# Normalising, projecting and attention in one program, a head's query tile ahead of its gate tile, and the first query tiles loaded under the last gate

## The chip, the core and the metric

The kernel runs on one core of a Trainium2 chip. The core has TensorE (PE, matmuls), VectorE (DVE), ScalarE (ACT), GpSimd (POOL) and SyncE (SP, which here only issues DMAs). Each engine runs its own instructions in order and waits for the others through semaphores. The metric is the device time of one execution in microseconds; the less the better.

## The reference

One inference step of a two-layer streaming encoder, for a prompt of 1024 tokens and a sample of 32 tokens behind 512 cached ones, with a model width of 1024. Layer 0 is what this change touches:

```python
hn = rmsnorm(h, norm_w[0])
q, k, v, z, qi, ki, wi = split_cols(hn @ w_in, ...)     # 8 query heads, 2 key heads, 8 index heads of 128
q, k, qi, ki = rope(q), rope(k), rope(qi), rope(ki)
score = einsum('bth,bths->bts', wi * IDX_SCALE, relu(qi . ki))   # one score per (token, key)
_, sel = top_k(where(admissible, score, -inf), n_sel)            # 256 keys (136 for the sample)
probs = softmax(where(valid, q . k[sel] * ATT_SCALE, -inf))
h = h + ((probs @ v[sel]) * silu(z)) @ w_out
```

Layer 1 is a gated linear recurrence with its own projections, and a last RMSNorm follows. Outputs are both groups' results, the keys, values and index keys, and the recurrent states. All is float32; each large product is made of three passes (high x high, high x low, low x high parts).

## The kernel before

Tokens lie in nine tiles of 128 (`NT` = 9, the last with the 32 sample tokens). The kernel is a series of programs, each an `nc.Block`, in which every engine has its own list of instructions. At the end of a block all engines wait for one another before the next begins. The first block, `norm_and_project`, runs `input_norm` and `attention_project`; the second is `attention`; the third, `out_and_recur`, is the output projection and the recurrence; the fourth is `final_out`.

`attention_project` goes through `TILES`, 27 column tiles of 128: index keys, 8 index queries, 2 key tiles, and then for each head a gate tile (`Z0`) and a query tile (`Q0`). A tile has three units of 352 tokens; a unit is one product of 24 matmuls into one of four PSUM banks (line 187). TensorE may start unit i when ScalarE has read unit i-4 (line 611), and VectorE too where it reads it. What happens to a unit depends on its kind:

- "gate": ScalarE applies Silu and writes it to `gT` (line 675).
- "q": ScalarE makes two half copies and one full one (lines 667, 668, 672; the full one waits until the store of the unit two before it has landed). GpSimd multiplies with sine and cosine (721, 724) and adds (710), the addition of a unit behind the multiplications of the next. SP then stores it to the DRAM tensor `q_rotated` (547).
- "rope" (index and key tiles): as "q", but VectorE multiplies with the cosine and the result stays in SBUF.

Between the two key tiles lie the "score" units. When the scores are there, VectorE searches the selection threshold of each token, bit by bit: `BITS` = 31 rounds of `search`, each of a proposal (line 802), counts over five tiles (793), and a decision (808, 809). The counts of the two widest tiles are made by ScalarE with Sign and an accumulator (`count_signs`, line 651), which waits for the proposal; the decision waits for both. `next_float` (821 to 834) ends the search. ScalarE's rounds stand in its instruction list among the reads of the units, at places that a table fixes when the program is built:

```python
BITS, PACE = 31, 6000
...
    if i > rope_last:
        time += 3850
        counted_after[i] = min(BITS, time // PACE)
```

`rope_last` is the last unit of the second key tile; 48 units, those of the gates and queries, follow it. After the first gate tile the key rows are also transposed and stored, one tile of tokens at every third unit (`rows_before`).

`attention` goes over 72 items (token tile, head). TensorE makes the logits (line 941) from the query tile, VectorE subtracts, masks and finds the minimum (`shift`, line 1027), ScalarE applies Exp (1067), VectorE divides (1035, 1037), TensorE transposes (954), ScalarE copies (1077), TensorE multiplies with the values (970), VectorE applies the gate (1043). SP loads the query tile of each token tile from `q_rotated` (line 913) into one of two places, tiles 0 and 1 at the block's start, a later tile t when the logits of tile t-2 are done; the raw output weights follow the load of tile 3 (918). These places lie in the region of `hn_lo`, which the projection reads to its end.

Of the kernel before, what the change touches and what calls it, by code (L numbers as in the profile page):

```python
# [25 lines left out]
P = 128  # L26
# [20 lines left out]

TILES = [KI0] + [QI0 + P * i for i in range(IH)] + [K0 + P * i for i in range(KVH)]
for _i in range(HEADS):
    TILES += [Z0 + P * _i, Q0 + P * _i]  # L50
RH, DK, DV = 8, 128, 128
REC_Q, REC_F, REC_V, REC_Z = range(4)

# [34 lines left out]
def build(nc, io):  # L88
    with ExitStack() as ctx:
# [42 lines left out]
        S["w_raw"] = space("w_raw", [P, W_SLOTS, KT, P])  # L132
        S["w_lo"] = Space(nc, w_at)("w_lo", [P, W_SLOTS, KT, P], F32R)
        S["w_hi"] = space("w_hi", [P, W_SLOTS, KT, P], F32R)
        S["cos"] = space("cos", [P, T])
        S["sin"] = space("sin", [P, T])

# [15 lines left out]
        S["raw_in"] = [sem(f"raw_in{i}") for i in range(W_SLOTS)]  # L153
        S["w_hi_done"], S["w_lo_done"] = sem("w_hi"), sem("w_lo")
        S["tables_in"], S["cache_in"] = sem("tables_in"), sem("cache_in")
        norm_and_project(nc, S, space)
        attention(nc, S)
        out_and_recur(nc, S)
        final_out(nc, S)

# [95 lines left out]
    return score[:, 0:PAST // P * 384].rearrange("p (b c) -> p b c", b=PAST // P)  # L256


def norm_and_project(nc, S, space):
    swapped = space("swapped", [P, 3, CW])  # L260
    relu = space("relu", [P, 2, 512])
    S["wi"] = space("wi", [P, NT, IH])
    S["kiTs"] = space("kiT_sample", [P, KEYS_S])
    S["signs"] = space("signs", [P, D], BF16)
    S["swapped"], S["relu"] = swapped, relu
    first, later = input_norm(nc, S), attention_project(nc, S)
    with nc.Block() as block:
        @block.sync
        def _(sp):
            first["sync"](sp)  # L270
            later["sync"](sp)

        @block.tensor
        def _(pe):
            first["tensor"](pe)
            later["tensor"](pe)

        @block.scalar
        def _(act):
            first["scalar"](act)  # L280
            later["scalar"](act)

        @block.gpsimd
        def _(pool):
            first["gpsimd"](pool)
            later["gpsimd"](pool)

        @block.vector
        def _(dve):
            first["vector"](dve)  # L290
            later["vector"](dve)


def input_norm(nc, S):
# [154 lines left out]
def attention_project(nc, S):  # L449
# [86 lines left out]
    if True:  # L536
        def sync(sp):
            def load(c):
                if c >= SLOTS:
                    sp.wait_ge(acc_ready, last_of_tile[c - SLOTS] + 1)  # L540
                sp.dma_start(raw[:, c % SLOTS], w_in[:, :, tiles[c]:tiles[c] + P]).then_inc(raw_in[c % SLOTS], 16)

            def store_q(c, parts):
                for i, (kind, tile, part, head) in enumerate(units):
                    if kind == "q" and tile == c and part in parts:
                        sp.wait_ge(rope_done, n_rope[i + 1])
                        sp.dma_start(q_dram[head, :, part * CW:(part + 1) * CW],
                                     relu[:, n_q[i] % 2, 0:CW]).then_inc(q_stored[n_q[i] % 2], 16)
# [12 lines left out]
            for c in range(SLOTS, len(tiles) + SLOTS):  # L561
                store_q(c - SLOTS, (0,))
                if c < len(tiles):
                    load(c)
                store_q(c - SLOTS, (1, 2))

                if c == SLOTS:
                    sp.wait_ge(v_read, NT)
                    sp.dma_start(io["v_prompt"][0, 0].rearrange("(t p) h d -> p t (h d)", p=P), v[:, 0:SAMPLE, :]).then_inc(v_stored, 16)
                    sp.dma_start(io["v_sample"][0, 0].rearrange("t h d -> t (h d)"), v[0:DEC, SAMPLE, :]).then_inc(v_stored, 16)  # L570
                for i in range(done, last_of_tile[c - SLOTS] + 1):
                    if i in rows_before:
# [300 lines left out]
def attention(nc, S):  # L873
# [29 lines left out]
    space = Space(nc, S["lo_at"])  # L903
    probs = space("probs", [P, RING, SEQ])
    low = space("low", [P, 3, N])
    q = space("q_tile", [P, 2, HEADS, P])
    with nc.Block() as block:
        @block.sync
        def _(sp):
# [11 lines left out]
        @block.gpsimd  # L921
        def _(pool):
# [4 lines left out]
        @block.tensor  # L927
        def _(pe):
            def multiply(i):
                t, h = items[i]  # L930
                n = keys(t)
# [2 lines left out]
                if i >= 2:  # L934
                    pe.wait_ge(logits_read, i - 1)
                if h == 0:
                    pe.wait_ge(q_in[t % 2], 16 * (t // 2 + 1))
                src = kTs if t == SAMPLE else kT
                for a in range(0, n, 512):
                    e = min(n, a + 512)  # L940
                    last = pe.matmul(logits[0:rows(t), i % 2, a:e], q[:, t % 2, h, 0:rows(t)],  # L941
                                     src[:, h // GROUP, a:e], start=True, stop=True)
                last.then_inc(logits_ready, 1)

# [13 lines left out]
            def mix(g, quarter):  # L958
# [8 lines left out]
                for j in range((n * quarter + 3) // 4, (n * (quarter + 1) + 3) // 4):  # L967
# [5 lines left out]
                    if j == n - 1:  # L973
                        last.then_inc(mixed, 1)

            for i in range(N + LAG + 4):
                if i < N:
                    multiply(i)
                if 0 <= i - LAG < N:
# [1 line left out]
                if i >= LAG + 4:  # L981
                    mix((i - LAG - 4) // 4, (i - LAG) % 4)

        @block.vector
        def _(dve):
            n_order = 0

            def link(instruction):
# [51 lines left out]
            def gate(g):  # L1040
# [3 lines left out]
                                  ps[2 + g % 2][:, 0:4 * rows(t)].rearrange("p (g q) -> p g q", g=4),  # L1044
                                  gT[:, h:h + 4, span(t)], ALU.mult).then_inc(gated, 1)

            for i in range(N + 12):
                if i < N:
                    t, h = items[i]
# [7 lines left out]
                if i >= 12 and i % 4 == 0:  # L1057
                    gate((i - 12) // 4)

        @block.scalar  # L1060
        def _(act):
            for i in range(N + LAG):
                if i < N:
                    t, h = items[i]
# [15 lines left out]
                if i in (6 * HEADS, 7 * HEADS):  # L1080
                    act.wait_ge(wo_in, 64)
                    out_weights_hi(act, S, i // HEADS - 6)


def out_and_recur(nc, S):
# [913 lines left out]
```

## Time and profile before

| | |
|---|---|
| median of 3 runs | 1477.39 us (1475.63 to 1477.44) |
| the profiled execution | 1477.57 us |
| its span, first to last instruction | 1475.8 us |
| TensorE busy / weight loads | 1386.3 us (94%) / 1204.5 us |
| VectorE, ScalarE, GpSimd busy | 926.5, 640.2, 553.7 us |
| mean granted TensorE clock | 0.983 of full |
| projection's last stage (gates and queries) | about 255 to 442 us |
| attention | about 456 to 650 us |

The times in the views are microseconds from the first instruction. Busy times are of compute instructions alone. The granted clock is 1.00 at 2.4 GHz and 0.50 at 1.2 GHz.

### The profile page before, as it was taken

What the parts mean: (1) busy time and instruction counts of PE and PEld (TensorE: products, weight loads), DVE (VectorE), ACT (ScalarE), POOL (GpSimd) and SP (SyncE); (2) the same over time, 40 slices, a digit from 0 to 9 for tenths busy, and PEclk for the clock granted to TensorE, in tenths of its full rate; (3) what the DMA queues carried; (4) which work ended last, traced back from release to release, by engine and by line L of the source; (5) the groups of instructions that cost most, each with busy time, mean ns of one, the idle gap of its engine ahead of it and who ended that gap; (6) DMA issues with size and microseconds to landing.
All of it is one profiled execution on the core that took longest, in us unless ns stands there. A gap on an engine that the chain in (4) does not pass through costs nothing. (4 is left out here: it accounts for less than half of the span.)

```text
span 1475.8 us, 21147 instructions
## 1 busy us (share of the span) xinstructions
PE 1386.3 (94%) x8028; PEld 1204.5 (82%) x8028; DVE 926.5 (63%) x1702; ACT 640.2 (43%) x1123; POOL 553.7 (38%) x399
## 2 busy tenths in 40 slices
PE   5999999999995999999989999999999999997998
PEld 5999746999993455458879998989898989996786
DVE  4211388869887988644568484848484848486233
ACT  4433365677764556531225352525252525252121
POOL 2466601464641001000025373737373737373000
PEclk9999999999997999999999999999999999999899
DMA  6211100223203310002231111111111111105221
GB/s 222 93 45 44 43 1 15 70 74 90 75 30 113 101 29 4 1 29 86 90 87 46 29 35 44 35 44 35 44 35 44 35 44 35 44 6 206 100 86 64
DMA packets 95316, 86.80 MB, mean 59 GB/s; under 512 B 5585, under 2 KB 83281, under 8 KB 95217
## 3 DMA queue, kind: packets, MB, share of 16 engines
q1 hardware_dynamic: 93584, 80.63, 17.6%
q0 software_dynamic: 1632, 4.82, 0.9%
q8 instruction: 66, 1.08, 0.3%
q14 instruction: 34, 0.27, 0.1%
HBM read 65.46 MB, written 19.97 MB: 58 GB/s over the span
## 5 line engine op out<-in xcount | busy, mean ns | idle before, releaser
L187 PE MATMUL bank<-hn_hi,rw_hi 128*128 128x352 f32 x768 | 251.1, 327 | 1.6 <-DVE hn_lo L177 1.6
L187 PE MATMUL bank<-hn_hi,rw_lo 128*128 128x352 f32 x768 | 247.8, 323 | 0.0
L187 PE MATMUL bank<-hn_lo,rw_hi 128*128 128x352 f32 x768 | 247.6, 322 | 0.0
L187 PE MATMUL bank<-hn_hi,w_hi 128*128 128x352 f32 x648 | 209.9, 324 | 0.0
L187 PE MATMUL bank<-hn_lo,w_hi 128*128 128x352 f32 x648 | 207.8, 321 | 0.0
L187 PE MATMUL bank<-hn_hi,w_lo 128*128 128x352 f32 x648 | 207.7, 321 | 0.0
L187 PEld LDWEIGHTS bank<-hn_hi,rw_hi 128*128 128x128 f32 x768 | 145.1, 189 | 3.5 <-issue 3.0
L187 PEld LDWEIGHTS bank<-hn_lo,rw_hi 128*128 128x128 f32 x768 | 145.5, 189 | 0.0
L187 PEld LDWEIGHTS bank<-hn_hi,rw_lo 128*128 128x128 f32 x768 | 145.1, 189 | 0.0
L721 POOL TENSOR_TENSOR swapped<-swapped,sin 128x352 f32<-128x352 f32 x57 | 53.9, 946 | 191.0 <-ACT swapped L668 125.9
L187 PEld LDWEIGHTS bank<-hn_hi,w_hi 128*128 128x128 f32 x648 | 121.6, 188 | 0.5 <-ACT relu L682 0.5
L187 PEld LDWEIGHTS bank<-hn_lo,w_hi 128*128 128x128 f32 x648 | 121.8, 188 | 0.0
L187 PEld LDWEIGHTS bank<-hn_hi,w_lo 128*128 128x128 f32 x648 | 121.5, 187 | 0.0
L793 DVE TENSOR_SCALAR_CACHE_REDUCE marks<-score,bits 128x384 bf16<-128x384 f32 (+5 forms) x157 | 117.1, 805 | 1.1
L1273 POOL TENSOR_TENSOR rw_lo<-rw_raw,rw_hi 128x1024 fp32r<-128x1024 f32 x32 | 95.7, 2994 | 43.9 <-ACT rw_hi L1266 43.8
L240 POOL TENSOR_SCALAR stats<-stats 128x1 f32<-128x1 f32 (+1 forms) x27 | 6.5, 240 | 280.2 <-ACT junk L1242 152.4
L1471 PE MATMUL wide<-levels 128*128 128x128 f32 (+1 forms) x832 | 98.0, 273 | 1.2 <-DVE last_state L1777 1.1
L1471 PEld LDWEIGHTS wide<-levels 128*128 128x128 f32 (+1 forms) x832 | 92.5, 185 | 6.7 <-issue 1.9
L1067 ACT ACTIVATE probs<-probs,low 128x128 f32<-128x128 f32 (+8 forms) x72 | 55.6, 772 | 87.8 <-DVE low L1027 87.4
L941 PE MATMUL wide<-kT,q_tile 128*128 128x512 f32 (+3 forms) x192 | 75.9, 509 | 14.6 <-DMA q_tile<-q_rotated 14.5
L1631 POOL TENSOR_TENSOR levels<-levels,k_rec 128x528 f32<-128x528 f32 (+1 forms) x48 | 89.0, 1879 | 1.4 <-ACT levels L1550 1.4
L1741 DVE TENSOR_TENSOR levels<-levels,q_rec 128x528 f32<-128x528 f32 (+1 forms) x48 | 87.5, 1886 | 0.0
(230 smaller groups left out, 2926.1 us busy)
## 6 DMA issues: line engine op xcount, KB each, us to landing
rw_raw<-in_rec_w_in SPq DMA_DIRECT2D x32, 512.0 KB, 4.0
w_raw<-in_att_w_in SPq DMA_DIRECT2D x27, 512.0 KB, 3.9
q_rotated<-relu SPq DMA_DIRECT2D x24, 176.0 KB, 1.8
xin<-in_x_prompt SPq DMA_DIRECT2D x8, 512.0 KB, 3.8
q_tile<-q_rotated SPq DMA_DIRECT2D x8, 512.0 KB, 3.8
wo_raw<-in_att_w_out SPq DMA_DIRECT2D x4, 1024.0 KB, 9.4
x_again<-in_x_prompt SPq DMA_DIRECT2D x8, 512.0 KB, 4.0
residual<-h_rows SPq DMA_DIRECT2D x8, 512.0 KB, 2.9
```

The lines of the kernel that those rows point to most:

```text
L187: last = pe.matmul(out, l, r, start=n == 0, stop=n == len(passes) - 1)
L240: pool.tensor_scalar(stats[0:r, 1, t:t + 1], stats[0:r, 0, t:t + 1], 1.0 / D, EPS, ALU.mult, ALU.add).then_inc(pool_order, 1)
L721: pool.tensor_tensor(swapped[:, r % 3, :], swapped[:, r % 3, :], sin[:, part * CW:(part + 1) * CW], ALU.mult).then_inc(sin_done, 1)
L793: step(dve.tensor_scalar(marks[0:r, i % 2, 0:keys(t)], tile(i, t), bound, 0.0, op, ALU.add, accum_out=counts[0:r, first + i:first + i + 1]))
L941: last = pe.matmul(logits[0:rows(t), i % 2, a:e], q[:, t % 2, h, 0:rows(t)], src[:, h // GROUP, a:e], start=True, stop=True)
L1067: act.activation(probs[0:r, i % RING, 0:n], probs[0:r, i % RING, 0:n], ACT.Exp, scale=-1.0, bias=low[0:r, 0, i:i + 1], accum_out=low[0:r, ...
L1273: pool.tensor_tensor(S["rw_lo"][:, slot], S["rw_raw"][:, slot], S["rw_hi"][:, slot].bitcast(F32), ALU.subtract).then_inc(S["rec_lo_done"], 1)
L1471: last = pe.matmul(out[:, 0:r], left, right, start=True, stop=True)
L1631: pool.tensor_tensor(x, x, level_view(k[:, slot], m)[:, :, 0, :], ALU.mult).then_inc(k_scaled, 1)
L1741: dve.tensor_tensor(x, x, level_view(q[:, slot], m)[:, :, 1, :], ALU.mult).then_inc(q_scaled, 1)
```

## The change

Three things are edited. The blocks of `norm_and_project` and `attention` become one, `project_and_attend`: every engine's list of the attention follows its list of the projection, with waits for what it needs of it in place of the wait at the block's end. In `TILES` the query tile of a head comes before its gate tile. The query tiles 0 and 1 get a place of their own, `q_first`, on top of the cosine and sine tables; SP loads them when all stores of the queries have landed. Tiles 2 and 3 are loaded into `q_tile` at the first logits. `PACE` is 5000 in place of 6000.

```diff
-    TILES += [Z0 + P * _i, Q0 + P * _i]
+    TILES += [Q0 + P * _i, Z0 + P * _i]
...
+        S["q_first"] = Space(nc, space.at)("q_first", [P, 2, HEADS, P])
         S["cos"] = space("cos", [P, T])
         S["sin"] = space("sin", [P, T])
...
-        norm_and_project(nc, S, space)
-        attention(nc, S)
+        project_and_attend(nc, S, space)
...
-    first, later = input_norm(nc, S), attention_project(nc, S)
+    stages = [input_norm(nc, S), attention_project(nc, S), attention(nc, S)]
     with nc.Block() as block:
         @block.sync
         def _(sp):
-            first["sync"](sp)
-            later["sync"](sp)
+            for stage in stages:
+                stage["sync"](sp)
... (the other four engines alike)
-    BITS, PACE = 31, 6000
+    BITS, PACE = 31, 5000
...
             for stored_q in q_stored:
                 sp.wait_ge(stored_q, 16 * n_q[N] // 2)
-            sp.wait_ge(v_stored, 32)
-            sp.wait_ge(stored[0], 32 * ((NT + 1) // 2))
-            sp.wait_ge(stored[1], 32 * (NT // 2))
+
+        def rows_stored(engine):
+            engine.wait_ge(stored[0], 32 * ((NT + 1) // 2))
+            engine.wait_ge(stored[1], 32 * (NT // 2))
...
+    q_in_first = [sem("q_in_first0"), sem("q_in_first1")]
+
+    def queries(t):
+        return (S["q_first"] if t < 2 else q_next)[:, t % 2]
...
             for t in range(NT):
-                if t >= 2:
+                if t == 2:
+                    sp.wait_ge(logits_ready, 1)
+                elif t >= 4:
                     sp.wait_ge(logits_ready, HEADS * (t - 1))
-                sp.dma_start(q[:, t % 2, :, 0:rows(t)],
-                             q_dram[:, :, span(t)].rearrange("h p t -> p h t")).then_inc(q_in[t % 2], 16)
+                sp.dma_start(queries(t)[:, :, 0:rows(t)],
+                             q_dram[:, :, span(t)].rearrange("h p t -> p h t")).then_inc(
+                                 q_in_first[t] if t < 2 else q_in[t % 2], 16)
                 if t == 3:
 
+                    sp.wait_ge(logits_ready, 2 * HEADS)
                     for ks, cols in weight_pieces():
                         sp.dma_start(S["wo_raw"][:, ks, cols], w_out[:, ks, cols]).then_inc(wo_in, 16)
+            S["rows_stored"](sp)
+            sp.wait_ge(S["v_stored"], 32)
             sp.wait_ge(wo_in, 64)
...
+            pe.wait_ge(S["k_rows_out"], NT)
+            pe.wait_ge(S["cache_out"], 3)
             for i in range(N + LAG + 4):
+                if i == LAG:
+                    pe.wait_ge(*S["units_read"])
+                    pe.wait_ge(*S["ropes_read"])
...
+            dve.wait_ge(S["open_done"], 3)
+            dve.wait_ge(*S["units_read"])
+            S["rows_stored"](dve)
```

## Rows read from the trace of the kernel before

**Rows 1.** The page, part 1: busy us, share of the span, instructions.

```profile
PE 1386.3 (94%) x8028; PEld 1204.5 (82%) x8028; DVE 926.5 (63%) x1702; ACT 640.2 (43%) x1123; POOL 553.7 (38%) x399
```

**Rows 2.** Windows: length, busy time of each engine, granted clock, DMA share, GB/s.

```profile
420.00:442.00 22.00, 21.73 (x137) 21.44 (x135) 18.75 (x51) 14.55 (x29) 9.71 (x10) 1.00 0.08 26
442.00:457.00 15.00, 0.75 (x3) 0.75 (x4) 9.07 (x32) 4.71 (x8) 4.00 (x6) 0.59 0.34 103
...
500.00:550.00 50.00, 47.77 (x197) 27.72 (x196) 45.62 (x103) 27.65 (x65) 0.00 (x0) 1.00 0.08 21
...
457.00:462.00 5.00, 5.00 (x21) 4.25 (x20) 4.04 (x28) 3.96 (x18) 0.00 (x0) 0.52 0.03 10
```

**Rows 3.** Timelines of the engines around the block's end: start, us, what, idle before.

```profile
430.38 0.47 ACT L675 ACTIVATE qiT_zT_gT<-bank 128x352 f32<-128x352 f32 x1 [0.89 <-PE bank L187]
...
441.81 0.45 ACT L667 COPY swapped<-bank 64x352 f32<-64x352 f32 x1
...
448.20 0.32 SPq L547 DMA_DIRECT2D q_rotated<-relu  x1
...
451.80 0.17 DVE L834 COPY_PREDICATED bits<-bits 128x7 uint32<-128x7 uint32 x1
...
452.47 1.28 ACT L1067 ACT_TABLE_LOAD   x1 [5.65 <-PEq L267]
...
452.48 1.00 SPq L913 DMA_DIRECT2D q_tile<-q_rotated  x2
...
456.25 3.17 PE L941 MATMUL wide<-kT,q_tile 128*128 128x128 f32 x10 [14.52 <-DMA q_tile<-q_rotated]
...
457.08 0.29 DVE L1027 CUSTOM_DVE_ANT_0 probs<-wide,open_mask 128x128 f32<-128x128 f32 x1 [5.11 <-PE wide L941]
```

**Rows 4.** The page, part 6: DMA issues, size, median us to landing.

```profile
q_rotated<-relu SPq DMA_DIRECT2D x24, 176.0 KB, 1.8
...
q_tile<-q_rotated SPq DMA_DIRECT2D x8, 512.0 KB, 3.8
```

**Rows 5.** Waits of SP's own queue, 400 to 480 us: total, times, longest.

```profile
SPq L267 <- PEq L267: 2.1, 1, 2.1
SPq L579 <- DMA q_rotated<-relu: 1.4, 1, 1.4
```

**Rows 6.** Timelines of ScalarE and VectorE: last key unit, first and late rounds.

```profile
255.40 0.45 ACT L667 COPY swapped<-bank 64x352 f32<-64x352 f32 x1 [2.90 <-PE bank L187]
...
263.21 0.16 DVE L802 TENSOR_SCALAR bits<-bits 128x7 uint32<-128x7 uint32 x1
...
426.45 0.17 DVE L808 TENSOR_TENSOR bits<-counts,select_state 128x7 uint32<-128x7 f32 x1
...
430.81 0.17 DVE L808 TENSOR_TENSOR bits<-counts,select_state 128x7 uint32<-128x7 f32 x1
...
446.92 0.40 DVE L808 TENSOR_TENSOR bits<-counts,select_state 128x7 uint32<-128x7 f32 x1 [0.33 <-ACT signs L651]
```

**Rows 7.** Groups of VectorE and ScalarE, 263.2 to 446.9 us: busy, mean ns, idle before.

```profile
L808 DVE TENSOR_TENSOR bits<-counts,select_state 128x7 uint32<-128x7 f32 x30 | 14.0, 468 | 29.8 <-ACT signs L651 29.2
L809 DVE COPY_PREDICATED bits<-bits 128x7 uint32<-128x7 uint32 x30 | 11.8, 393 | 1.0
L802 DVE TENSOR_SCALAR bits<-bits 128x7 uint32<-128x7 uint32 x31 | 9.6, 309 | 1.0
...
L651 ACT ACTIVATE signs<-score,bits 128x896 bf16<-128x896 f32 (+1 forms) x62 | 68.0, 1096 | 7.7 <-DVE bits L802 6.4
```

**Rows 8.** Timelines of GpSimd and VectorE, 300 to 306 us.

```profile
302.60 2.39 POOL L216 TENSOR_TENSOR w_lo<-w_raw,w_hi 128x1024 fp32r<-128x1024 f32 x1
...
303.16 1.85 DVE L808 TENSOR_TENSOR bits<-counts,select_state 128x7 uint32<-128x7 f32 x1 [0.49 <-ACT signs L651]
```

**Rows 9.** Timeline of ScalarE in the recurrence: a table load and what follows.

```profile
773.46 1.28 ACT L1525 ACT_TABLE_LOAD   x1
774.75 0.82 ACT L1525 ACTIVATE k_rec<-bank 128x352 f32<-128x352 f32 x2
```

More of the change, by code:

```diff
@@ L256, in cached_keys, with project_and_attend @@
     return score[:, 0:PAST // P * 384].rearrange("p (b c) -> p b c", b=PAST // P)
-def norm_and_project(nc, S, space):
+def project_and_attend(nc, S, space):
     swapped = space("swapped", [P, 3, CW])
@@ L269, in _ @@
         def _(sp):
-            first["sync"](sp)
-            later["sync"](sp)
+            for stage in stages:
+                stage["sync"](sp)
         @block.tensor
         def _(pe):
-            first["tensor"](pe)
-            later["tensor"](pe)
+            for stage in stages:
+                stage["tensor"](pe)
         @block.scalar
         def _(act):
-            first["scalar"](act)
-            later["scalar"](act)
+            for stage in stages:
+                stage["scalar"](act)
         @block.gpsimd
         def _(pool):
-            first["gpsimd"](pool)
-            later["gpsimd"](pool)
+            for stage in stages:
+                stage["gpsimd"](pool)
         @block.vector
         def _(dve):
-            first["vector"](dve)
-            later["vector"](dve)
+            for stage in stages:
+                stage["vector"](dve)
 def input_norm(nc, S):
@@ L576, in sync @@
                 sp.wait_ge(stored_q, 16 * n_q[N] // 2)
-            sp.wait_ge(v_stored, 32)
-            sp.wait_ge(stored[0], 32 * ((NT + 1) // 2))
-            sp.wait_ge(stored[1], 32 * (NT // 2))
+        def rows_stored(engine):
+            engine.wait_ge(stored[0], 32 * ((NT + 1) // 2))
+            engine.wait_ge(stored[1], 32 * (NT // 2))
+        S["rows_stored"], S["v_stored"], S["open_done"], S["cache_out"] = rows_stored, v_stored, open_done, cache_out
+        S["units_read"], S["ropes_read"], S["k_rows_out"] = (act_read, n_act[N]), (dve_read, n_dve[N]), k_out
         def tensor(pe):
@@ L905, in attention, with wait_queries, sync, gpsimd @@
     low = space("low", [P, 3, N])
[L906 to L909, printed above, removed]
+    q_next = space("q_tile", [P, 2, HEADS, P])
+    q_in_first = [sem("q_in_first0"), sem("q_in_first1")]
+    def queries(t):
+        return (S["q_first"] if t < 2 else q_next)[:, t % 2]
+    def wait_queries(engine, t):
+        if t < 2:
+            engine.wait_ge(q_in_first[t], 16)
+        else:
+            engine.wait_ge(q_in[t % 2], 16 * (t // 2))
+    if True:
+        def sync(sp):
             for t in range(NT):
-                if t >= 2:
+                if t == 2:
+                    sp.wait_ge(logits_ready, 1)
+                elif t >= 4:
                     sp.wait_ge(logits_ready, HEADS * (t - 1))
-                sp.dma_start(q[:, t % 2, :, 0:rows(t)],
-                             q_dram[:, :, span(t)].rearrange("h p t -> p h t")).then_inc(q_in[t % 2], 16)
+                sp.dma_start(queries(t)[:, :, 0:rows(t)],
+                             q_dram[:, :, span(t)].rearrange("h p t -> p h t")).then_inc(
+                                 q_in_first[t] if t < 2 else q_in[t % 2], 16)
                 if t == 3:
+                    sp.wait_ge(logits_ready, 2 * HEADS)
                     for ks, cols in weight_pieces():
                         sp.dma_start(S["wo_raw"][:, ks, cols], w_out[:, ks, cols]).then_inc(wo_in, 16)
+            S["rows_stored"](sp)
+            sp.wait_ge(S["v_stored"], 32)
             sp.wait_ge(wo_in, 64)
-        @block.gpsimd
-        def _(pool):
+        def gpsimd(pool):
             pool.tensor_copy(kTs[:, :, PAST:], kT[:, :, SEQ:T]).then_inc(keys_done, 1)
@@ L925, in _, with tensor @@
                 out_weights_lo(pool, S, c)
-        @block.tensor
-        def _(pe):
+        def tensor(pe):
             def multiply(i):
@@ L936, in multiply @@
                 if h == 0:
-                    pe.wait_ge(q_in[t % 2], 16 * (t // 2 + 1))
+                    wait_queries(pe, t)
                 src = kTs if t == SAMPLE else kT
@@ L940, in multiply @@
                     e = min(n, a + 512)
-                    last = pe.matmul(logits[0:rows(t), i % 2, a:e], q[:, t % 2, h, 0:rows(t)],
+                    last = pe.matmul(logits[0:rows(t), i % 2, a:e], queries(t)[:, h, 0:rows(t)],
                                      src[:, h // GROUP, a:e], start=True, stop=True)
@@ L982, in _, with vector @@
                     mix((i - LAG - 4) // 4, (i - LAG) % 4)
-        @block.vector
-        def _(dve):
+        def vector(dve):
             n_order = 0
@@ L1058, in _, with scalar @@
                     gate((i - 12) // 4)
-        @block.scalar
-        def _(act):
+        def scalar(act):
             for i in range(N + LAG):
@@ L1082, in _ @@
                     out_weights_hi(act, S, i // HEADS - 6)
+    return dict(sync=sync, tensor=tensor, scalar=scalar, gpsimd=gpsimd, vector=vector)
 def out_and_recur(nc, S):
```

## The prediction

> **What bounds the kernel now.** I read the page first. TensorE is busy for 94% of the span [rows 1], so over the whole kernel the question is where it stands still, and for whom. The windows come next [rows 2]. Until 442 us TensorE is busy for 21.73 of 22 us. From 442 to 457 us it is busy for 0.75 of 15 us. In the attention stage (500 to 550 us) VectorE is busy for 45.62 of 50 us: there VectorE, and not TensorE, sets the pace. The reader is to see one hole, between the projection and the attention, with a different engine as the bound on either side of it. The chain of waits that ends last holds only the tail of the kernel and says nothing of this place.
>
> Third comes the timeline around the hole [rows 3]. TensorE's first logits matmul starts at 456.25 us after 14.52 us of idling, so its last projection matmul ended at 441.73. Four things happen in these 14.5 us. ScalarE reads the last query unit (from 441.81), GpSimd rotates it, and SP issues its store at 448.20. The store lands some 1.8 us later [rows 4]: SP's own waits show 1.4 us for it and then 2.1 us at the block's end [rows 5]. VectorE writes the last word of the search at 451.80 and ends at 451.97; only then does the block end, and at 452.47 to 452.48 ScalarE and SP start the next one. So the block's end waited for VectorE, not for the store. Last, the query tile is issued at 452.48 and used at 456.25, 3.77 us later; rows 4 have 3.8 as its median landing. VectorE's first attention operation is at 457.08.
>
> Two things are late here, then: the search (until 451.97), and a store and a load in series that begin only when the last projection unit is done.
>
> Fourth, why the search is late. Its rounds run on VectorE and ScalarE together. A round without a wait takes 430.81 - 426.45 = 4.36 us [rows 6]. From 263.2 to 446.92 us, 183.7 us, there are 31 rounds, 5.93 us each, with 29.2 us of it (30 of the 31) waiting for ScalarE's signs [rows 7]. Without that wait a round is (183.7 - 29.2) / 31 = 4.98 us. The small operations on `bits` hold the rest above 4.36: they took 14.0 + 11.8 + 9.6 = 35.4 us, where 91 of them at 0.17 us would be 15.5.
>
> **The change, part by part.**
>
> Order of the tiles. A query tile has three units, its gate tile three. The last query unit now ends where the last gate unit ends today. ScalarE reads that one at 430.38 and the last query unit at 441.81 [rows 3], so the last query chain moves forward by 11.43 us: store issued at 448.20 - 11.43 = 436.8, landed at 438.6, query tile issued at about 438.7, landed 3.77 us later at 442.5. Its two loads into `q_first` come before any wait on the logits. SP passes nothing new before them: the last row stores stand seventeen units from the end, and the weight loads are out. TensorE's own work is the same number of units, so it is free at 441.73 as now. The first logits matmul starts at the later of the two, 442.5 us. Gain: 456.25 - 442.5 = 13.7 us, if VectorE is there.
>
> The search with PACE 5000. The table gives round n to the first unit k after the last rotated key unit with 3.85 k >= 5 n. All 31 are placed by k = 41 (with 6000 only 30 are placed by k = 48, and the last runs behind all units). Units end on average (441.73 - 255.4) / 48 = 3.88 us apart, since ScalarE reads the last key unit at 255.40 [rows 3, 6]; k = 41 is at 414.5 us. ScalarE then needs a read and the two counts, some 3.5 us: 418. VectorE's own bound is 263.2 + 31 x 4.98 = 417.6. The tail of the search was 451.97 - 446.92 = 5.05 us. So it ends at about 423 us, and even 10 us of coupling would leave it 9 us before the first logits. What was the last to come is then covered by the gate units. If that cover were gone (the search as late as now), VectorE would begin at 452.1 and the gain would be 5.0 us only.
>
> Does the denser table hold up TensorE? ScalarE must propose a round no faster than VectorE finishes one. Places of the rounds are (414.5 - 263.2) / 30 = 5.04 us apart, VectorE needs 4.98: balanced. Where four units in a row carry a round, four rounds of 4.36 us stand against 15.5 us of units, 2 us late. ScalarE's share: it is busy for 14.55 of 22 us now [rows 2], 66%, and its sign passes are 68.0 / 31 = 2.2 us a round [rows 7], 37% at a round each 5.93 us; at one each 5.04 us they are 44%, so ScalarE is busy for about 73%. TensorE may run ahead of ScalarE by three units (four banks), 11.6 us. I cost this at nothing, with 0 to 3 us as bounds.
>
> Port between VectorE and GpSimd. A 0.17 us comparison took 1.85 us from 303.16 to 305.01, just until GpSimd's 2.39 us subtraction from 302.60 ended at 304.99 [rows 8]. The number of GpSimd operations does not change, so this stays inside the 4.98. By the Trainium skill (SBUF — State Buffer, section on two separate sides) the pair's port is an exclusive lock held for the whole instruction; the trace agrees, and a rule that every round must lose the rest of such a burst would make the search at most 31 x 0.9 = 28 us longer by an estimate from the 2.39 us row, 9 us too late. The sum doesn't rest on it.
>
> One program instead of two. The wait at the block's end goes: 451.97 to 452.47, and with it the order "search, then query load". Both are in the sum. ScalarE's table load for the exponential was hidden at 452.47. Now it comes behind the last gate read, 442.3 to 443.6, and the first exponential is wanted at about 443.4: 0.1 to 0.2 us, which only the first items see. A load takes 1.28 us, and the operation behind one starts with no further gap (773.46 + 1.28 = 774.74, next at 774.75) [rows 9]. The Trainium skill (ScalarE: Activation LUTs, section "What ACT_TABLE_LOAD costs") adds about 1.38 us of draining, which these rows do not show; by it the first exponential would come 1.4 us later and the gain would be about 1 us less. Sign now stands before the first Silu; at present the two alternate all through the search with no load in between, so at worst one 1.28 us load is added, in ScalarE's slack. The new waits of VectorE and TensorE (rows stored, units read, keys out) are on things done before or at 442.3 us, so nothing queues behind them. The loads of query tiles 2 and 3 go out at the first logits, earlier than now, and the weight load behind them keeps its place: nothing.
>
> The clock. During the hole and just behind it the granted clock is low: 0.59 from 442 to 457 us and 0.52 from 457 to 462 us, then 1.00 [rows 2]; that is 1.2 GHz against 2.4. Without the hole TensorE comes straight from dense work. In 457 to 462 us VectorE idled for 0.96 of 5 us, mostly waiting for logits; and the first logits took 0.83 us to reach VectorE. At the full clock I take 0.3 us from the latter and 0.4 from the former: 0.7 us, bounds 0 and 1.5. The attention is VectorE's afterwards, so a faster TensorE brings no more.
>
> Sum: 13.7 + 0.7 - 0.1 = 14.3 us. Everything behind the first logits hangs on them and shifts with them. The profiled execution took 1477.57 us (span 1475.8 and 1.8 around it), so it becomes 1463.3; the median of the runs lies 0.2 us below it, which gives 1463.1 us.
>
> **The rivals.**
> A. The last load or ScalarE's reading comes later, or the gates wait a little: for instance a query load that lands 2 us behind its median or a ScalarE lag of more than 11.6 us by a few. Gain 5 to 11.5 us: 1466 to 1472.4. For it: the packed ScalarE. Against it: no rounds stand in the last seven units.
> B. The search stays as late as now, because the port and not the pace holds it: gain 5.0 us, 1472.4. Against it: 29.2 us of idling for ScalarE are visible and only 9.5 are needed.
> C. Slower. The rounds keep their 5.93 us although ScalarE is told to start them every 5. The 31st is then proposed at 263.2 + 30 x 5.93 = 441 us, 26.5 us behind its unit; ScalarE, which stands in count_signs, leaves the banks unread, and TensorE stops for 26.5 - 11.6 = 15 us. Against the 14.3 that is 1478 us. It decides from 5.9 us a round on; below 5.4 us nothing is lost. Against it: without its waits a round is at 4.98.
> D. No change: the attention's later items absorb the shift. Nothing in them waits for a fixed time, so I see no way but an unseen stall.
> E. More gain: the dips of the clock that follow fall elsewhere, 2 to 4 us more: 1459 to 1461.
>
> **How the numbers follow.** Forecast (gain 11.5 to 16.5) 0.74, A 0.10, B 0.04, C 0.04, D 0.03, E 0.05. A measurement of this kernel tells about 0.2%, 3 us, from no change. Faster: forecast, A, B and E, 0.93; same: D, 0.03; slower: C, 0.04. The range runs from 1459.5, for most of E, to 1468.5, which holds the nearer half of A: about 0.84 in all.
>
> **What would show it.** Right: TensorE's idle before the first logits about 1 us, released by the query tile's load; first logits at 442 to 443 us; the last `bits` operation of the search at 421 to 432 us; VectorE's wait for ScalarE's signs below 15 us; TensorE busy without gaps from 263 to 441 us; granted clock 1.00 around the first logits; one table load between the last gate read and the first exponential. Wrong: gaps of TensorE in the projection with ScalarE's reads as releaser (C, A), the search's last operation behind 440 us (B), more table loads between Silu and Sign, or a first attention tile as slow as now.

## The result and the profile after

The changed kernel takes 1469.16 us in the median (1468.99 to 1470.45, 4 runs), against 1477.26 us before in the same comparison: a ratio of 0.9948, interval 0.9934 to 0.9962. That is 8.1 us faster, where 14.3 us were forecast, and 0.7 us above the top of the stated range. The direction was right and the size was not.

The profiled execution took 1469.18 us with a span of 1467.4 us. Its timelines around the place where the block's end was, as in [rows 3] (line numbers are those of the new kernel: 655 is ScalarE's sign pass, 671, 672 and 676 its three copies of a query unit, 679 the gate, 812, 813 and 806 VectorE's operations on `bits`, 928 the query load, 958 the logits, 1048 VectorE's first attention operation):

```profile
427.28 1.04 ACT L655 ACTIVATE signs<-score,bits 128x896 bf16<-128x896 f32 x1 [0.16 <-DVE bits L806]
...
430.22 0.45 ACT L671 COPY swapped<-bank 64x352 f32<-64x352 f32 x1
...
433.87 0.45 ACT L671 COPY swapped<-bank 64x352 f32<-64x352 f32 x1 [0.88 <-PE bank L187]
...
438.70 0.45 ACT L676 COPY relu<-bank 128x352 f32<-128x352 f32 x1 [3.91 <-DMA q_rotated<-relu]
...
445.35 0.46 ACT L679 ACTIVATE qiT_zT_gT<-bank 128x352 f32<-128x352 f32 x1 [3.35 <-PE bank L187]
...
445.83 1.28 ACT L1090 ACT_TABLE_LOAD   x1
...
442.01 1.22 SPq L547 DMA_DIRECT2D q_rotated<-relu  x2
...
444.82 1.00 SPq L928 DMA_DIRECT2D q_first<-q_rotated  x2
...
435.63 0.66 DVE L838 COPY_PREDICATED bits<-bits 128x7 uint32<-128x7 uint32 x1
449.65 0.29 DVE L1048 CUSTOM_DVE_ANT_0 probs<-wide,open_mask 128x128 f32<-128x128 f32 x1 [13.36 <-PE wide L958]
...
449.01 0.68 PE L958 MATMUL wide<-kT,q_first 128*128 128x128 f32 x4 [3.70 <-DMA q_first<-q_rotated]
```

The 14.52 us hole is gone. In its place stand 3.70 us of waiting for the query load, and the first logits begin at 449.01 us, 7.2 us earlier than at 456.25. The search is over at 436.3, long before. But the last query tile's first unit is read only at 430.22 and its third at 433.87, the third's full copy waits for 3.91 us for a store, and the last gate unit is read at 445.35 where the last unit of the kernel before was read at 441.81. Both of the times that the forecast took as given, TensorE's end and the query chain, are late.

The waits of the projection's last stage, 255 to 445 us (us in total, times, longest):

```profile
ACT signs L655 <- DVE bits L806: 31.5, 21, 2.7
...
ACT relu L676 <- DMA q_rotated<-relu: 9.8, 5, 3.9
...
PEld bank L187 <- ACT relu L676: 3.1, 2, 2.0
DVE bits L812 <- ACT signs L655: 3.0, 2, 2.0
PE bank L187 <- ACT relu L676: 2.5, 2, 1.7
...
PEld bank L187 <- ACT qiT_zT_gT L679: 1.1, 1, 1.1
PE bank L187 <- ACT qiT_zT_gT L679: 0.8, 1, 0.8
```

VectorE's 29.2 us of waiting for ScalarE [rows 7] have become 3.0. ScalarE now waits for VectorE's proposals, 31.5 us where it was 6.4. And TensorE, which had no gap here, stands still for 2.5 + 0.8 = 3.3 us for banks that ScalarE has not read, 4.2 us by its weight loads (3.1 + 1.1), which stop a little sooner. The second is what it costs: from the read of the last key unit to the read of the last gate unit are 190.6 us (254.72 to 445.35), and from key unit to last unit were 186.4 before. VectorE's groups, 263.2 to 431.1 us, as in [rows 7]:

```profile
L813 DVE COPY_PREDICATED bits<-bits 128x7 uint32<-128x7 uint32 x30 | 23.0, 766 | 1.0
L806 DVE TENSOR_SCALAR bits<-bits 128x7 uint32<-128x7 uint32 x31 | 13.6, 440 | 1.0
...
L812 DVE TENSOR_TENSOR bits<-counts,select_state 128x7 uint32<-128x7 f32 x31 | 9.5, 306 | 4.4 <-ACT signs L655 3.0 <-DVE marks L797 0.4
```

The three small operations take 46.1 us, against 35.4 before. The counts (line 797, 793 before), which are the bulk of a round, take 114.7 us in both kernels. The windows (length, busy times, granted clock, DMA share, GB/s) show where TensorE lost its 3.3 us, and that its clock stayed up across the seam, 0.89 where [rows 2] had 0.59:

```profile
380.00:420.00 40.00, 38.47 (x240) 37.90 (x238) 38.08 (x92) 28.89 (x53) 19.64 (x17) 1.00 0.17 48
420.00:442.00 22.00, 20.23 (x125) 19.95 (x126) 15.54 (x47) 12.78 (x26) 13.74 (x15) 1.00 0.15 47
442.00:457.00 15.00, 10.61 (x52) 8.45 (x50) 6.01 (x38) 6.90 (x25) 1.07 (x2) 0.89 0.57 164
```

The missing time adds up at the first logits, 449.01 against the 442.5 of the forecast. The third unit was read at 433.87, not 430.38: 3.5 us (the 4.2 us of TensorE, less 0.7 us by which this execution had reached the stage earlier). The wait before its full copy was 3.9 us, where before it was 1.35 (the row below, of the kernel before): 2.6 us. Load to first matmul took 449.01 - 444.82 = 4.2 us, not 3.8: 0.4 us. Together 6.5 of 6.5 us.

```profile
444.07 0.45 ACT L672 COPY relu<-bank 128x352 f32<-128x352 f32 x1 [1.35 <-DMA q_rotated<-relu]
```

### The profile page after: what moved, and what is told of

It is laid out like the page before. It is cut to its first block and busy times, and to the rows that moved or that the text cites. A ratio compares the mean times of both kernels' runs of the same rounds, so it can differ in the third digit from the quotient of the medians.

```text
span 1467.4 us, 21141 instructions
## 1 busy us (share of the span) xinstructions
PE 1383.5 (94%) x8028; PEld 1201.1 (82%) x8028; DVE 936.4 (64%) x1702; ACT 641.2 (44%) x1123; POOL 554.9 (38%) x399
## 5 line engine op out<-in xcount | busy, mean ns | idle before, releaser
L655 ACT ACTIVATE signs<-score,bits 128x896 bf16<-128x896 f32 (+1 forms) x62 | 68.0, 1097 | 32.8 <-DVE bits L806 31.5
```

What stands on the lines that cost most here:

```text
L655: act.activation(signs[0:rows(t), 0:keys(t)], score[0:rows(t), at[t]:at[t] + keys(t)], ACT.Sign, bias=bits[0:rows(t), (step + 1) % 2, i:i ...
```

## The experiments

Theory P in the expectations: GpSimd's bursts hold VectorE's small operations, so that a round costs 5.3 us when VectorE does not wait for ScalarE; the denser table makes ScalarE wait for VectorE, and this holds up TensorE and the last query chain. The rivals: O, the order of the tiles does it; L, ScalarE has too much work; T, the pace is all and the last tile's chain adds nothing. "First logits" is the start of TensorE's first attention matmul that found its query tile.

| kernel | ratio to before (interval) | TensorE's gaps | search ends | first logits |
|---|---|---|---|---|
| before | | none | 452.0 | 456.25 |
| changed | 0.9948 (0.9934 to 0.9962) | 3.3 us | 436.3 | 449.01 |
| PACE 6000 | 0.9968 (0.9955 to 0.9981) | none | 449.0 | 442.09, VectorE at 449.10 |
| PACE 5500 | 0.9942 (0.9927 to 0.9956) | none | 443.5 | 445.70 |
| less cosine work | 0.9901 (0.9885 to 0.9918) | none | 424.5 | 440.53 |
| before with PACE 5000 | 1.0003 (0.9994 to 1.0013) | 2.5 us | 438.7 | 457.64 |
| PACE 5250 | 0.9956 (0.9935 to 0.9978) | none | 440.9 | 448.74 |
| PACE 5250, hold | 0.9940 (0.9921 to 0.9960) | none | 444.0 | 446.40 |
| gate first, PACE 5500 | 0.9991 (0.9967 to 1.0014) | none | 439.5 | 453.28 |
| three slots, PACE 5000 | 0.9931 (0.9904 to 0.9957) | 4.4 us | 437.0 | 446.81 |
| three slots, PACE 5500 | 0.9918 (0.9903 to 0.9933) | none | 442.4 | 444.58 |
| three slots, PACE 5300, hold | 0.9902 (0.9885 to 0.9918) | none | 439.0 | 441.61 |

Ratios are each to the kernel before on the same chip. "None" means that TensorE was busy without a gap from 255 to 440 us. The last key unit, ahead of the part that was changed, was read between 253.9 and 254.7 us in the ten kernels of one program and at 255.4 and 255.6 in the two with two blocks. The cause was not looked for. So up to 0.8 us of a difference between first logits of the former, and up to 1.5 us against the kernel before, lies ahead of the changed part. On the chip of the second group, PACE 5250 to three slots with PACE 5000, all times were higher and wider (the kernel before at 1482.59 us), so their intervals are wide. Their medians (1472.36, 1472.86, 1478.84 and 1471.93 us) cannot be held against the times in the expectations, and they are judged below by the profiles' first logits.

**PACE back at 6000.**

```diff
-    BITS, PACE = 31, 5000
+    BITS, PACE = 31, 6000
```

> The changed kernel with PACE back at 6000, all else as changed. Theory P (GpSimd's bursts hold VectorE's small operations, so a round costs 5.3 us when VectorE does not wait for ScalarE; the denser table then makes ScalarE wait, which holds up the projection and the last query chain): at 6000 TensorE ends the projection at about 441.7 us without gaps, the query tile is there at 442 to 443.5, but the search ends only at about 450 to 452, so VectorE begins there: gain 5 to 7 us over the kernel before, 1470.5 to 1472.5. Theory O (the order of the tiles itself delays ScalarE and the last queries): gaps of TensorE in the projection stay at about 3 us and the query tile lands near 449 as with 5000, so the time is that or worse, 1472 to 1475. Theory L (ScalarE has simply too much work per unit at the faster pace): as P here.

1472.34 us, 4.4 us off the kernel before. Its timelines (first matmuls of the attention; VectorE around the end of the search; SP):

```profile
442.09 0.68 PE L958 MATMUL wide<-kT,q_first 128*128 128x128 f32 x4 [1.26 <-DMA q_first<-q_rotated]
449.45 0.80 PE L958 MATMUL wide<-kT,q_first 128*128 128x128 f32 x2 [6.68 <-DVE low L1048]
```

```profile
448.78 0.17 DVE L838 COPY_PREDICATED bits<-bits 128x7 uint32<-128x7 uint32 x1
449.10 0.29 DVE L1048 CUSTOM_DVE_ANT_0 probs<-wide,open_mask 128x128 f32<-128x128 f32 x1 [0.15 <-DVE bits L838]
```

The reader is to see the cover of the prediction taken away: the query tile is there and the first logits stand at 442.09 us, as forecast to 0.4 us, and VectorE comes 7 us later, straight from the search. With the slow table the projection and the query chain are as the sum had them, to within 1 us. Theory O falls: the order alone makes no gap and no late chain. VectorE's groups, 262 to 455 us:

```profile
L813 DVE COPY_PREDICATED bits<-bits 128x7 uint32<-128x7 uint32 x31 | 13.4, 434 | 1.1
L812 DVE TENSOR_TENSOR bits<-counts,select_state 128x7 uint32<-128x7 f32 x31 | 12.8, 412 | 29.8 <-ACT signs L655 28.7 <-DVE marks L797 0.4
...
L806 DVE TENSOR_SCALAR bits<-bits 128x7 uint32<-128x7 uint32 x31 | 8.7, 282 | 1.0
```

This kernel and the changed one differ in the pace alone. With it VectorE waits for 28.7 us in place of 3.0, and the small operations take 34.9 us in place of 46.1; a round without the waits is (444.81 - 262.30 - 28.7) / 31 = 4.96 us. One thing more stands here: with VectorE late, the table load came only at 449.48, and the first exponential waited for its end at 450.77, so the load was in the way for 1.3 us.

**PACE 5500.** One number again, 5500.

> The changed kernel with PACE 5500. Theory P: the places of the rounds, 5.54 us apart, are a little wider than VectorE's 5.33 us, so ScalarE waits little, TensorE has no gap, the search ends at about 436 to 440 us, the first logits come at 442 to 444 us: 1462.5 to 1465. Theory O: the chain of the last queries is as late as with 5000, first logits at 447 to 449: 1467 to 1469. Theory L: ScalarE's load falls only by a tenth: gaps of TensorE of 1 to 2 us stay and the time is about 1466 to 1467.

1468.01 us, and no theory has all of it. TensorE's gaps are gone, as P said, but the time is 3 us above P's span, the first logits come at 445.70 us and not at 442 to 444, and the search ends at 443.5 and not at 436 to 440. The time lies within what O expected, whose first logits (447 to 449) are not seen and which fell with PACE 6000. L expected gaps, and there are none. ScalarE's timeline shows what is left:

```profile
426.97 1.04 ACT L655 ACTIVATE signs<-score,bits 128x896 bf16<-128x896 f32 x1 [1.98 <-DVE bits L806]
...
435.49 0.46 ACT L676 COPY relu<-bank 128x352 f32<-128x352 f32 x1 [3.77 <-DMA q_rotated<-relu]
```

A round stands between the first and the second unit of the last query tile. ScalarE waits for its proposal until 426.97 and then reads the second and third unit back to back. GpSimd adds the sine part of a unit only behind the multiplications of the next, so the first unit is stored late, and the third copy, which has the first one's slot, waits 3.77 us. The late store is a cost of its own beside TensorE's gaps.

**Less work on GpSimd.** The cosine multiplication of the query units on 8 of 352 columns.

```diff
-                    pool.tensor_tensor(rotated(i), rotated(i), cos[:, part * CW:(part + 1) * CW],
+                    pool.tensor_tensor(rotated(i)[:, 0:8], rotated(i)[:, 0:8], cos[:, part * CW:part * CW + 8],
```

> The changed kernel (PACE 5000) in which GpSimd multiplies only 8 of the 352 columns of a query unit by the cosine, so that most of that multiplication is left out and GpSimd's bursts are 0.8 us shorter each (24 of them). Theory P: VectorE's small operations take 8 to 15 us less in all, a round goes from 5.33 to about 4.9 to 5.05 us, ScalarE's waits for the proposals fall from 31.5 to below 22 us, TensorE's gap goes, and the last store is also earlier: first logits at 441.5 to 444 us, 1461 to 1465. Theory O: only the chain gets 1 to 2 us shorter: 1467 to 1468. Theory L: ScalarE's work is unchanged, so TensorE's gaps of 3.3 us stay: about 1467.

1462.02 us, within what P expected; O and L had 1467 or more. The first logits are 1 us ahead of P's span. VectorE's groups from 262 to 446 us:

```profile
L813 DVE COPY_PREDICATED bits<-bits 128x7 uint32<-128x7 uint32 x31 | 18.8, 608 | 1.1
...
L812 DVE TENSOR_TENSOR bits<-counts,select_state 128x7 uint32<-128x7 f32 x31 | 7.2, 234 | 8.2 <-ACT signs L655 7.2
L806 DVE TENSOR_SCALAR bits<-bits 128x7 uint32<-128x7 uint32 x31 | 6.1, 196 | 1.0
```

The small operations, on which nothing was edited, take 32.1 us in place of 46.1, and a round without the waits is (420.32 - 262.17 - 7.2) / 31 = 4.87 us. ScalarE's waits for the proposals fall from 31.5 to 16.2 us, with all its own work still there, so it was not overloaded (L falls), and TensorE has no gap at PACE 5000. That the rounds are longer because of GpSimd is shown by this run. It does not divide its gain between the rounds and the shorter query chain, which it also helps.

**The pace alone.** The kernel before, two blocks, gate first, PACE 5000.

> The kernel before with PACE 5000 alone: two blocks, gate tile first. Theory P: the search ends at about 434 to 437 us, TensorE gets the same gaps of about 3 us, and the block's end now waits for the last store, which lands 3 us later than before, at 452 to 453.5 us, against 451.97 for the search before: 1477 to 1479.5, no gain at all. Theory O (the gaps come from the new order): no gaps, the block ends at about 450.3 us: 1475.5 to 1476. Theory L: as P.

1477.18 us, ratio 1.0003: no gain, as P expected. The search ends at 438.7 us, 13 us earlier than before though 1.7 us later than P's span, TensorE has gaps of 2.5 us, and the block ends at 453.9 instead of 452.5 because the last store is later by what TensorE lost; the first logits are at 457.64. VectorE's lead is worth nothing while the block's end stands between it and the query load.

**PACE 5250, and the same without a round among the last query tile's reads.** The second has, behind the table of rounds:

```diff
+    last_q = last_of_tile[len(tiles) - 2]
+    for i in (last_q - 2, last_q - 1):
+        counted_after[i] = counted_after[last_q - 3]
```

> The changed kernel with PACE 5250. Theory P: the places of the rounds are 5.29 us apart against VectorE's 5.33, so ScalarE runs 1 to 3 us behind and TensorE has no gap or one below 1 us, but the 29th to 31st round still stand among the reads of the last query tile or right before it, so the two-slot wait (a copy that waits until the store of the unit two before it has landed) stays at 2 to 4 us and the first logits come at 445 to 447 us: 1466 to 1468. Rival T (the pace is all, the last query tile's own chain costs nothing of its own): 1463 to 1464.5.

> As the kernel with PACE 5250, but with no round among the reads of the last query tile: what would stand behind its first two units comes behind its third. Theory P: its three copies follow TensorE, the two-slot wait is back at 0.6 to 1.5 us, the last store at about 437 to 438.5, first logits at 442 to 444 us, the search ends at about 437 to 440 us: 1462.5 to 1465. Rival T: as the kernel without the hold, within 1 us.

The first logits at 448.74 us are 2 us later than P's numbers, with no gap of TensorE: the wait before the third copy is 3.78 us. With the hold they are at 446.40, 2.3 us earlier, but the wait is 4.20 us and the hope of 442 to 444 is a miss. ScalarE's timeline of the second says why:

```profile
425.19 1.04 ACT L658 ACTIVATE signs<-score,bits 128x896 bf16<-128x896 f32 x1 [2.75 <-DVE bits L809]
...
428.12 0.45 ACT L674 COPY swapped<-bank 64x352 f32<-64x352 f32 x1
...
436.02 0.46 ACT L679 COPY relu<-bank 128x352 f32<-128x352 f32 x1 [4.20 <-DMA q_rotated<-relu]
```

ScalarE is already late when it comes to the last query tile, since it waited for the round ahead of it; it reads the three units back to back, and two slots don't allow that. To keep rounds out of these reads is not enough. Rival T falls in both runs: the last query tile's chain costs time though TensorE has no gap, and the hold moves the first logits by 2.3 us.

**Gate tile first, PACE 5500**, all else of the change kept.

> The changed kernel with the gate tile ahead of the query tile again, and PACE 5500. The last query chain then begins only with TensorE's last unit. Theory P and the prediction's sum: TensorE ends at about 441.7, last store at about 448.2, landed at 450, query tile issued at 450 to 450.5 and there at 454 us: gain of 2 to 3 us from the block's end alone, 1474 to 1475.5. Rival O (the order costs as much as it brings): 1468 to 1470.

The profile has the first logits at 453.28 us with 12.42 us of idle before them; the last two stores are issued together at 446.4 to 447.6 and the query load at 449.18. Its execution took 1475.11 us and the ratio is 0.9991 (0.9967 to 1.0014). So at the first logits the order is worth 453.28 - 445.70 = 7.6 us at this pace, which rival O had at nothing, and one program without the order 456.25 - 453.28 = 3.0 us. The times don't resolve these 3 us: the interval holds 1.

**Three slots.** The query units go to DRAM from three slots in place of two, with a third semaphore.

```diff
-    relu = space("relu", [P, 2, 512])
+    relu = space("relu", [P, 3, 512])
...
-        return relu[:, n_q[i] % 2, 0:CW] if kind == "q" else target[:, part * CW:(part + 1) * CW]
+        return relu[:, n_q[i] % 3, 0:CW] if kind == "q" else target[:, part * CW:(part + 1) * CW]
...
-                        if n_q[i] >= 2:
-                            act.wait_ge(q_stored[n_q[i] % 2], 16 * (n_q[i] // 2))
+                        if n_q[i] >= 3:
+                            act.wait_ge(q_stored[n_q[i] % 3], 16 * (n_q[i] // 3))
```

> The changed kernel (PACE 5000) with three slots in place of two for the query units on their way to DRAM, so that a copy waits for the store three units before it. Theory P, by its sum of the delay (3.5 us from TensorE's gaps, 2.6 us from the two-slot wait of 3.9 us, 0.4 us from the load): the wait of 3.9 us goes and the last store follows the read; TensorE's gaps stay or shrink by the 0.9 us that part of them owes to this wait: first logits at 445.5 to 447 us, bound by TensorE's own end: 1465.5 to 1467. Rival T: nothing, since all the delay is ScalarE's wait for the proposals: 1469.

First logits at 446.81 us, as expected, 2.2 us earlier than with two slots (0.6 us of it ahead of the stage) and now with only 0.84 us of waiting for the load: TensorE's own end, with gaps of 3.3 + 1.1 = 4.4 us, is the bound. The two-slot wait is gone and rival T falls. One part of P is a miss: the gaps grew from 3.3 to 4.4 us, where they were to stay or shrink. VectorE's small operations take 49.6 us in place of 46.1 and ScalarE waits for the proposals for 38.7 us in place of 31.5, so the rounds are a little longer still. In the profiled execution 100 us of the recurrence (1100 to 1200 us) had TensorE busy for 93.0 us at a granted clock of 0.98, where the kernel with three slots and PACE 5500 has 95.8 us at 1.00, so its total hides part of the gain; I have no cause for that.

**Three slots with PACE 5500, and with PACE 5300 and the hold.**

> Three slots for the query units and PACE 5500, all else as changed. Theory P: both parts of the delay are then gone. TensorE has no gap and ends at about 441 us; the last query unit's copy follows its read, the last store is issued at 437 to 438 us, the query tile is there at 443 to 444 us; the search, no longer behind the copy that waited, ends at 439 to 441.5 us: gain of 12.5 to 13.5 us over the kernel before, ratio 0.9909 to 0.9915, first logits at 443 to 444 us. Rival T: as PACE 5500 with two slots, first logits at 445.5 us, ratio 0.994.

> Three slots, PACE 5300 and no round among the reads of the last query tile. Theory P: the 30th round's proposal comes at about 425 us, and ScalarE, which stands before it, reads the last query tile's first unit only at 427 to 428 us; TensorE has no gap; the last store at 436.5 to 438 us, first logits at 442.5 to 444 us, ratio 0.9907 to 0.9917, within 1 us of the kernel with PACE 5500 and three slots. Rival T: first logits at 445 to 447 us, ratio 0.993 to 0.995.

With PACE 5500 the first logits are at 444.58 us (ratio 0.9918), 0.6 us behind the expected span, and the search ends at 442.4, 0.9 us behind its own: a round still stands between the reads of the last query tile. With the hold at PACE 5300 the first logits are at 441.61, 0.9 us ahead of P's span, so the two kernels are 3 us apart at this place and not within 1 us. The kernel with the hold is also a little faster than P's ratio, at 1461.50 us, ratio 0.9902 (0.9885 to 0.9918). This is faster than the changed kernel, and by 15.7 us than the one before. Timelines of TensorE, SP and ScalarE in it:

```profile
441.61 0.68 PE L961 MATMUL wide<-kT,q_first 128*128 128x128 f32 x4 [1.39 <-DMA q_first<-q_rotated]
```

```profile
431.77 3.94 SPq L550 DMA_DIRECT2D q_rotated<-relu  x3
437.31 1.00 SPq L931 DMA_DIRECT2D q_first<-q_rotated  x2
```

```profile
428.81 0.45 ACT L674 COPY swapped<-bank 64x352 f32<-64x352 f32 x1 [0.33 <-PE bank L187]
429.28 0.45 ACT L675 COPY swapped<-bank 64x352 f32<-64x352 f32 x1
429.74 0.46 ACT L679 COPY relu<-bank 128x352 f32<-128x352 f32 x1
```

ScalarE catches up with TensorE on the third unit, the copy waits for nothing, and the query load goes out 7.5 us earlier than in the changed kernel. One window over the projection, and one over the seam:

```profile
442.00:457.00 15.00, 11.98 (x52) 7.14 (x51) 13.37 (x65) 9.32 (x40) 0.00 (x0) 1.00 0.28 78
263.00:440.00 177.00, 177.00 (x1122) 176.68 (x1120) 169.95 (x417) 131.26 (x237) 97.75 (x86) 1.00 0.27 75
```

TensorE is busy for all of the 177 us, and the seam has the full clock. With two slots the hold brought 2.3 us and left the chain late; here ScalarE reads the three units in a row and no copy waits. Against the kernel with three slots and PACE 5500 the pace was changed together with the hold, so the runs don't say how much of the 3 us is the hold's.

These two kernels also bound what a slow round costs. Their small operations take 53.1 and 52.2 us, more than in the changed kernel, a round without the waits is 5.54 and 5.49 us, and ScalarE waits for the proposals for 37.4 and 33.5 us. Yet TensorE has no gap. It is not the sum of ScalarE's waits that costs, but how late ScalarE is at a single read.

## Why the prediction was wrong

**What was right.** The search was the last to come at the block's end; with the shorter pace it ends ahead of the first logits, at 436.3 us, though 13 us later than the forecast 423, and the cover absorbed that; the order moves the query chain; and with the chain moved, a sound run stands at 442.09 us for the first logits (PACE 6000) against 442.5 forecast (its stage had begun 0.9 us earlier than in the kernel before). The three slots with the hold (441.61) and less cosine work (440.53) also get there. In those two runs the gain is 15.7 and 14.8 us of a forecast 14.3.

**The step that failed** is "Without that wait a round is (183.7 - 29.2) / 31 = 4.98 us". It took VectorE's waits for ScalarE off and left the rest alone. But the waits and GpSimd's bursts were cover for each other: a burst that fell in one of VectorE's waits cost nothing then, and falls on a small operation now. The timelines of the two engines over the 31 rounds show it. Before, GpSimd was busy in 22.2 of the 29.5 us that VectorE waited for ScalarE, and 20 of the 93 small operations took over 0.25 us; now VectorE waits for 3.0 us and 30 of the 93 are that long, 29 of them ending within 0.1 us of a GpSimd operation (before, 17 of the 20). Of the 26 us that VectorE waited less, about 11 us came back in these operations (35.4 to 46.1 us), and a round costs (431.02 - 262.54 - 3.0) / 31 = 5.34 us. The kernel with PACE 6000, where only the pace is put back, has its waits and its 4.96 us a round again. Two rows of the changed kernel, GpSimd's and VectorE's timelines, show one such burst:

```profile
277.95 2.39 POOL L216 TENSOR_TENSOR w_lo<-w_raw,w_hi 128x1024 fp32r<-128x1024 f32 x1 [4.44 <-ACT w_hi L209]
```

```profile
277.97 2.40 DVE L813 COPY_PREDICATED bits<-bits 128x7 uint32<-128x7 uint32 x1
```

The operation is a 0.17 us one elsewhere, and ends with GpSimd's. The Trainium skill (SBUF — State Buffer, section on two separate sides) has the shared port as an exclusive lock held for the whole instruction; the trace agrees, and the run with less cosine work bears it out. The prediction cited this rule and said "this stays inside the 4.98", because the number of bursts does not change. The number did not; what they fall upon did.

**The steps that hung on it.** "Balanced", 5.04 against 4.98 us, should have read 5.04 against 5.34: ScalarE falls behind by 0.3 us a round, 9 us by the 31st, and unevenly on top: the proposal of the 31st came at 427.1 us, 12.6 us behind the 414.5 at which the forecast placed its unit, and TensorE can run ahead by three units, 11.6 us. The loss of TensorE was costed at nothing with 3 us as its bound; it was 4.2 us. The prediction's own signs of being wrong had this one, gaps with ScalarE's reads as releaser, and it is what came. Rival C stated the mechanism and had nothing lost below 5.4 us a round, which was a little too high. Its size was wrong here: at 5.34 us the delay costs part of the gain and not all of it. Nor is 5.34 us a fixed price: a round without the waits took 4.87 to 5.54 us in the twelve kernels, by how the bursts fell.

**What the sum left out.** The query chain was shifted as one piece by 11.43 us, with its 1.4 us wait for the store. When ScalarE is late and reads two or all three of the units back to back, that wait becomes 3.8 to 4.2 us, in four kernels. Rival A is what came about: it named ScalarE's reading as late, its 1466 to 1472.4 us hold the measured time, it had a chance of 0.10, and said against itself "no rounds stand in the last seven units". This is true of the table and does not help: the 31st round stands behind k = 41 and the last query tile begins at k = 43, and ScalarE reached the last query tile only after the proposal of the 31st, at 427.1 us.

**Smaller terms.** The table load cost nothing: it ended at 447.1, before the first exponential was wanted. Where the exponential was wanted at once, it began 0.01 us after the load (in the kernel with PACE 6000 the load ran from 449.48 to 450.76 and the exponential began at 450.77). The Trainium skill (ScalarE: Activation LUTs, section "What ACT_TABLE_LOAD costs") adds 1.38 us of draining; none of these rows shows it. The forecast took 0.7 us for the clock. Measured: VectorE's first operation moved by 7.43 us, 0.2 us more than the first logits, and the span by 8.4, so about 1 us came behind it; how much of this is the clock's is not shown. Of the 7.43, 0.7 us was there before the changed part: the last key unit was read at 254.72 us, against 255.40 [rows 6]. The 0.9 us a round in the prediction's estimate on the port has no row behind it, and nothing hung on it. Terms below 1 us are not resolved.

## What to carry to other kernels

Idle time that is taken from one engine is not all gained: ask what else was hidden in it, and cost each instruction that shares a port or a queue with another engine as if it had no cover. When two engines work in turns, a schedule a little faster than the slower one doesn't just stop helping; the other engine stands in the wait with everything that is queued behind it, and the delay comes out where a short buffer meets it. With enough slack in the buffers the same waiting costs nothing. Before moving a chain of copies, stores and loads as one piece, check whether its buffers still suffice when its units arrive in a row.

## What the runs showed of the hardware

- A VectorE operation on 128x7 values, 0.17 us by itself, took up to 2.40 us beside a 2.39 us GpSimd subtraction that had started 0.02 us earlier. Over 31 rounds such operations took between 34.9 us (PACE 6000) and 53.1 us (three slots, PACE 5500) with the same instructions on both engines, by how GpSimd's bursts fell on them, and 32.1 us with shorter bursts. The counts of the same rounds, each of a whole tile of scores, were not lengthened: 114.7 us before and after.
- A store to DRAM and a load of it in series took 1.8 us to landing and then 3.7 to 4.3 us from the load's issue to the first matmul (two 512 KB loads issued together). The short end is that of the two kernels with a block's end ahead of the load; in one program it was 4.1 to 4.3 us. The runs don't say why.
